# Local-attention mixer: scores as two whole-array fp32r passes on split, stacked heads instead of one plain f32 matmul per half array

## The reference, cut to what matters

```
q = q.reshape(B, nb, BLOCK, SW_KV_HEADS, G, SW_DIM)
kb, vb = band(k), band(v)                    # previous block and this one
s = einsum('bnqgrd,bnkgd->bngrqk', q, kb) * (SW_DIM ** -0.5) + bias
s = where(valid, s, NEG)
p = softmax(concatenate([s, sink], axis=-1), axis=-1)[..., :-1]
o = einsum('bngrqk,bnkgd->bnqgrd', p, vb)
```

## Time and profile before

| | us |
|---|---|
| median of three runs | 2695.01 |
| lowest, highest | 2693.04, 2697.74 |
| profiled execution: span, first to last instruction | 2693.6 |
| mean granted TensorE clock in it | 0.997 of full speed |
| local-attention mixer, from the first score to the last value product | 1585.3 to 1700 |
| the eight tiles' scores begin at | 1585.29, 1598.96, 1615.17, 1627.35, 1639.55, 1651.99, 1664.18, 1676.62 |

### The profile page before, as it was taken

How to read it: one execution, slowest core, us unless ns; L and a number is a source line. 1 busy time by engine, 2 the same in 40 slices (tenths; PEclk the granted TensorE clock), 3 DMA queues, 4 the chain that set the end, 5 groups by cost and what they waited for, 6 DMA issues and landing times.

```text
span 2693.6 us, 32187 instructions
## 1 busy us (share of the span) xinstructions
PE 2653.5 (99%) x12935; PEld 2126.5 (79%) x12935; DVE 1460.7 (54%) x2615; ACT 1122.8 (42%) x1521; POOL 1167.0 (43%) x880
## 2 busy tenths in 40 slices
PE   8999999999999999999999999999999999999998
PEld 7787677778888877778888876888888777888887
DVE  5888556657554145657554145575522565575522
ACT  4544544444333236653333236443333344443332
POOL 3454443335445532335445541354455332454453
PEclk9999999999999999999999999999999999999999
DMA  4224032222223221112223331222233222222232
GB/s 164 79 94 172 1 133 86 70 73 96 106 96 110 104 88 63 63 65 98 104 94 110 109 110 48 79 94 98 106 109 110 94 87 71 94 94 94 94 122 81
DMA packets 46597, 253.44 MB, mean 94 GB/s; under 512 B 4528, under 2 KB 11200, under 8 KB 18928
## 3 DMA queue, kind: packets, MB, share of 16 engines
q1 hardware_dynamic: 35376, 231.92, 24.3%
q10 hardware_dynamic: 11072, 19.47, 2.2%
HBM read 249.21 MB, written 10.55 MB: 96 GB/s over the span
## 4 chain that ended last, share of the span: by engine, by line
PE 92%; DVE 4%; ACT 2%; POOL 1%; issue 1%; DMA 0%; SPq 0%; DVEq 0%; ACTq 0%
PE ring L481 79%; PE ring L978 3%; PE turn L983 2%; PE turn L481 1%; PE out L1022 1%; POOL wlo L1219 1%; PE ring L776 1%; PE ring L645 1%; PE out L792 1%; DVE sp L2238 1%; PE out L1028 0%; DVE e L2206 0%; PE out L1110 0%; ACT whi L1270 0%; DVE z L2241 0%
## 5 line engine op out<-in xcount | busy, mean ns | idle before, releaser
L1219 POOL TENSOR_TENSOR wlo<-raw,whi 128x512 fp32r<-128x512 f32 x840 | 1121.8, 1367 | 1456.9 <-ACT whi L1270 1456.8
L481 PE MATMUL ring<-xh,whi 128*128 128x512 f32 x1888 | 753.4, 399 | 9.3 <-DVE xl L1753 8.4
L481 PE MATMUL ring<-xh,wlo 128*128 128x512 f32 x1888 | 736.6, 390 | 0.0
L481 PE MATMUL ring<-xl,whi 128*128 128x512 f32 x1888 | 736.5, 390 | 0.0
L1270 ACT ACTIVATE whi<-raw 128x2048 fp32r<-128x2048 f32 x215 | 411.3, 1914 | 437.1 <-DMA raw<-in_pieces 421.8
L481 PEld LDWEIGHTS ring<-xh,whi 128*128 128x128 f32 x1888 | 354.9, 188 | 114.9 <-issue 41.1
L481 PEld LDWEIGHTS ring<-xh,wlo 128*128 128x128 f32 x1888 | 354.9, 188 | 75.3
L481 PEld LDWEIGHTS ring<-xl,whi 128*128 128x128 f32 x1888 | 355.2, 188 | 72.3 <-issue 3.4
L2391 DVE SCALAR_TENSOR_TENSOR taps<-u,conv,taps 128x511 f32<-128x511 f32 (+1 forms) x344 | 295.7, 905 | 17.3 <-ACT taps L1695 14.8
L2405 DVE TENSOR_TENSOR u<-ring,r 128x512 f32<-128x512 f32 x168 | 114.4, 687 | 299.7 <-PE ring L481 299.7
L481 PE MATMUL ring<-hh,whi 128*128 128x512 f32 (+1 forms) x693 | 265.3, 383 | 0.0
(11 more groups left out here) (304 smaller groups left out, 3423.0 us busy)
## 6 DMA issues: line engine op xcount, KB each, us to landing
raw<-in_pieces SPq DMA_DIRECT2D x215, 1024.0 KB, 4.8
toep<-diag_store ACTq DMA_DIRECT2D x16, 512.0 KB, 3.6
diag_store<-diag_row ACTq DMA_DIRECT2D x1, 5120.0 KB, 25.6
band_store<-band_row ACTq DMA_DIRECT2D x1, 3072.0 KB, 33.1
h<-in_x SPq DMA_DIRECT2D x4, 512.0 KB, 6.3
wbias<-band_store ACTq DMA_DIRECT2D x4, 512.0 KB, 7.2
raw<-in_pieces SPq DMA_DIRECT2D x4, 256.0 KB, 6.4
result<-h SPq DMA_DIRECT2D x2, 512.0 KB, 3.0
```

Source lines behind the costliest of these rows:

```text
L481: ins = pe.matmul(out, stationary, moving, start=first and n == 0, stop=last and n == 2)
L1219: ins = pool.tensor_tensor(m.wlo[slot][:, part], m.raw[slot][:, part], m.whi[slot][:, part].bitcast(F32), ALU.subtract)
```

## The change

The scores become f32r matmuls over the whole array. For each key head `kd[g]` holds two arrays: its high part, in both partition halves, and its low part, in both halves. For each query head there is one array `qw`: its high part in the head's own partition half, its low part in the other half. Head j's block is then two passes with the same stationary query array, one on the high keys and one on the low keys, summed in PSUM over all 128 partitions.

VectorE takes the keys in one operation a unit into `kn`, ScalarE rounds high parts (2 operations of 64x512 for each key head and each tile's queries), VectorE subtracts for the low parts (again 2 and 2). TensorE waits for `q_low` and `k_low` instead of `pu_taken`. The query arrays of even and odd tiles are kept apart. Tiles 0 and 1 begin after 33 and 46 quanta instead of 30 and 44.

```diff
-          "window": (30, 44, 60, 68, 76, 84, 92, 100)}
+          "window": (33, 46, 60, 68, 76, 84, 92, 100)}
...
-        self.kd = self.at("kd", [P, 4, S], o + 36864)
+        self.kd = [self.at(f"kd{g}", [P, 2, S], o + (36864, 40960, 88064, 92160)[g], F32R) for g in range(4)]
+        self.qw = [[self.at(f"qw0{j}", [P, S], o + 14336 + 16384 * j, F32R) for j in range(2)],
+                   [self.at(f"qw1{j}", [P, S], sq_at + 2048 * j, F32R) for j in range(2)]]
...
+        self.kn = [self.at(f"kn{u}", [P, S], o + 49152 + 3584 * (2 + u)) for u in range(2)]
...
+    def stacked_pair(b, t, i, qs, ks, lo, n):
+
+        for j in range(2):
+            u = 8 * t + 2 * i + j
+            if u < 2:
+                pe.wait_ge(m["unit_taken"], b.at("unit_taken", 0))
+            else:
+                pe.wait_ge(m["su_taken"], b.at("su_taken", u - 1))
+            out, q = m.ring[2 + j][:, 0:n], qs[j][:, i * P:(i + 1) * P]
+            pe.matmul(out, q, ks[:, 0, lo:lo + n], start=True, stop=False)
+            pe.matmul(out, q, ks[:, 1, lo:lo + n], start=False, stop=True).then_inc(m["su_ready"], 1)
...
-                pe.wait_ge(m["pu_taken"], b.at("pu_taken", WINDOW_Q_UNIT[t] + 1))
+                pe.wait_ge(m["q_low"], b.at("q_low", 2 * t + 2))
+                pe.wait_ge(m["k_low"], b.at("k_low", 2 * (t // 2) + 2))
...
-                    score_pair(b, t, i, m.qt[t % 2], m.kd[:, t // 2, :], lo, n)
+                    stacked_pair(b, t, i, m.qw[t % 2], m.kd[t // 2], lo, n)
...
+        def keys_high(g):
+            act.wait_ge(m["pu_taken"], b.at("pu_taken", g // 2 + 1))
+            for to in range(2):
+                act.activation(m.kd[g][64 * to:64 * to + 64, 0, :], m.kn[g // 2][64 * (g % 2):64 * (g % 2) + 64, :],
+                               ACT.Copy).then_inc(m["k_high"], 1)
+
+        def queries_high(t):
+            act.wait_ge(m["pu_taken"], b.at("pu_taken", WINDOW_Q_UNIT[t] + 1))
+            if t >= 2:
+                act.wait_ge(m["su_ready"], b.at("su_ready", 8 * t - 8))
+            for j in range(2):
+                half = slice(64 * j, 64 * j + 64)
+                act.activation(m.qw[t % 2][j][half, :], m.qt[t % 2][half, :], ACT.Copy).then_inc(m["q_high"], 1)
         split_hi(b, 2)
+        keys_high(0)
+        queries_high(0)
         split_hi(b, 3)
+        keys_high(1)
...
+            if t == 0:
+                keys_high(2)
+                keys_high(3)
             hi_at(b, "window", t, 1)
+            if t + 1 < TILES and t != 1:
+                queries_high(t + 1)
             if 2 <= t:
                 take_out(b, t - 2)
             if 1 <= t < TILES + 1:
                 weights(2 * t - 2)
                 weights(2 * t - 1)
+            if t == 1:
+                queries_high(t + 1)
             hi_at(b, "window", t, 2)
...
-                for g in range(2):
-                    src = slice(64 * g, 64 * g + 64)
-                    for to in range(2):
-                        ins = dve.tensor_tensor(m.kd[64 * to:64 * to + 64, 2 * unit + g, :], project_bank(m, unit)[src, :],
-                                                m.r[src, :], ALU.mult)
...
+                take_feature(b, unit, m.kn[unit], 1.0)
+
+        def keys_low(g):
+            dve.wait_ge(m["k_high"], b.at("k_high", 2 * g + 2))
+            half = slice(64 * (g % 2), 64 * (g % 2) + 64)
+            for to in range(2):
+                dve.tensor_tensor(m.kd[g][64 * to:64 * to + 64, 1, :], m.kn[g // 2][half, :],
+                                  m.kd[g][half, 0, :].bitcast(F32), ALU.subtract).then_inc(m["k_low"], 1)
+
+        def queries_low(t):
+            dve.wait_ge(m["q_high"], b.at("q_high", 2 * t + 2))
+            for j in range(2):
+                half, other = slice(64 * j, 64 * j + 64), slice(64 - 64 * j, 128 - 64 * j)
+                dve.tensor_tensor(m.qw[t % 2][j][other, :], m.qt[t % 2][half, :],
+                                  m.qw[t % 2][j][half, :].bitcast(F32), ALU.subtract).then_inc(m["q_low"], 1)
...
         for unit in range(3):
             take(unit)
+        keys_low(0)
+        queries_low(0)
...
             if t == 0:
                 take(3)
+                keys_low(1)
...
             if t < TILES and t != 1:
                 take(t + 5 if t else 4)
+            if t == 0:
+                keys_low(2)
+                keys_low(3)
+                queries_low(1)
             if 1 <= t < TILES + 1:
                 normalise(2 * t - 1)
             if t == 1:
                 take(6)
+            if 1 <= t < TILES - 1:
+                queries_low(t + 1)
             if 2 <= t:
                 take_low(b, t - 2)
```

More of the change, by code:

```diff
@@ L205, in mix @@
         else:
+            t.update(q_high=16, q_low=16, k_high=8, k_low=8)
             t.update(exped=64, sunk=16, lsum=16, rl_ready=16, normed=64)
@@ L2280, in take @@
             else:
-                dve.wait_ge(m["pu_ready"], b.at("pu_ready", unit + 1))
-                for g in range(2):
-                    src = slice(64 * g, 64 * g + 64)
-                    for to in range(2):
-                        ins = dve.tensor_tensor(m.kd[64 * to:64 * to + 64, 2 * unit + g, :], project_bank(m, unit)[src, :],
-                                                m.r[src, :], ALU.mult)
[L2287 to L2290, removed]
+                take_feature(b, unit, m.kn[unit], 1.0)
[11 more added lines that the diff above has]
+                                  m.qw[t % 2][j][half, :].bitcast(F32), ALU.subtract).then_inc(m["q_low"], 1)
         def normalise(h):
```

## The result

The changed kernel takes 2698.69 us (median of 20 runs, 2695.49 to 2701.25) against 2695.16 (20 runs, 2691.51 to 2697.74): a ratio of 1.0014, 95% interval 1.0008 to 1.0021. So it is slower by about 3.5 us, 0.14%, which is under the 0.2% taken as the bound of no change. Forecast were 2696.5 us, no change within 0.2%, and a range of 2687.5 to 2702.5. The case forecast was the right one; the step from it to the number was 2.2 us short.

A forecast was written before the change was run, and what follows sets the result against it. TensorE, busy for 99% of the span, was taken as the bound; a 10.8 us gain against 12.35 us of added waits gave +1.5 us on 2695.0, so 2696.5 us, with an 8-in-10 range of 2687.5 to 2702.5.

The forecast's parts named there:

- The case forecast: Local-attention mixer: TensorE's saving is taken back by waits on other engines, 2696.5 us; chance 0.45.
- gain of TensorE, eight tiles: Score pairs in the mixer: shorter f32r passes save 1.28 us a tile, 10.2 us over eight tiles.
- wait of tile 0 that goes: Tile 0: TensorE's 0.55 us wait for VectorE goes, as eight key copies become two.
- tile 0, piece 2: Before tile 0's scores: three VectorE subtractions delay GpSimd's low part of piece 2, costing 1.0 us.
- tile 1, its query: Before tile 1's scores: TensorE waits for ScalarE's queued copies and VectorE's query subtractions beside GpSimd, costing 3.4 us.
- tile 2, its query: Before tile 2's scores: take, copies and subtractions of its query end late, costing 1.0 us.
- ScalarE's queue, five tiles: Tiles 2 to 6: query copies delay ScalarE's output and transposes copy, 0.85 us a tile, 4.25 in five.
- GpSimd, tiles 2, 4, 6: Tiles 2, 4, 6: the earlier normalisation falls under GpSimd's operations and takes turns with them, costing 2.7 us.
- rival B: Score passes: 128-column f32r runs like plain f32, 0.21 us instead of 0.12, giving 2701.1 us; chance 0.18.
- rival C: Wait before tile 1: TensorE's clock falls, 3.4 us at half costs 1.7, giving 2698.2 to 2699.9; chance 0.12.
- Rival A: Mixer waits stay small, 5.2 us at their low ends, giving 2689.4 us; chance 0.23.
- Rival D: Score passes don't do what is said: one with its bank free still waits for its weights; chance 0.02.

The follow-up runs named there:

- the run with no split: Kernel before with two f32r passes per score block, keys and queries not split into high and low parts: 2687.24 us, ratio 0.9969.
- the starts alone: Kernel before with only tiles 0 and 1 begun after 33 and 46 quanta instead of 30 and 44: 2695.86 us, ratio 0.9996.
- tile 1's query first: Changed kernel with tile 1's query split ahead of the keys of tiles 4 to 7 and piece 4, on ScalarE and VectorE: 2694.66 us, ratio 0.9998.
- three edits: Changed kernel with tile 1's queries first, query high parts of tiles 3 to 7 on VectorE, high parts of pieces 6 and 7 sooner: 2688.02 us.
- tile 1 four quanta later: Changed kernel with tile 1 begun after 50 quanta instead of 46, tiles 2 to 6 one quantum later: 2697.5 us, ratio 1.0006.
- the query's high part on VectorE: Changed kernel with query high parts of tiles 3 to 7 made by VectorE instead of ScalarE: 2692.95 us, ratio 0.9993.
- GpSimd's work moved: Changed kernel with ScalarE making high parts of pieces 6 and 7 one tile earlier, so GpSimd's low parts come sooner: 2695.1 us, ratio 1.0003.

## Why the prediction was right, and where it was short

The forecast's balance was 12.35 of costs against 10.8 of gain. Term by term, with what the trace after and the runs show:

| term | forecast, us | measured, us | where |
|---|---|---|---|
| gain of TensorE, eight tiles | 10.2 | 10.3 | the run with no split, its waits added |
| wait of tile 0 that goes | 0.55 | 0.5 to 0.8 | the starts alone: the stage 0.76 shorter |
| tile 0, piece 2 | 1.0 | 1.1 | wait of 0.95, 1.1 between starts |
| tile 1, its query | 3.4 | 2.8 | wait of 2.65, 2.8 between starts |
| TensorE's clock behind it | 0 | 1.5 | 3.4 us at half; tile 1's query first gives the same |
| tile 2, its query | 1.0 | 1.0 | wait of 0.80, 0.96 between starts |
| ScalarE's queue, five tiles | 4.25 | 5.1 | between starts: 1.07, 0.99, 1.08, 0.90, 1.08 |
| GpSimd, tiles 2, 4, 6 | 2.7 | 2.5 | between starts: 0.43 + 1.30 + 1.28 - 0.5 |
| balance | +1.5 | +2.9 to +3.2 | the stage: +3.25 |

"Between starts" is the time from TensorE's last start before the wait to the first behind it, less what the same step takes with no wait; it is 0.06 to 0.17 us more than the wait that the profile names.

**The gain** came out as its steps had it. The value taken for a 128-column pass, 0.12 us, is 0.11 in the trace; the bound of 0.21 wasn't met, and with it rival B fell: the steps at the two ends of the first pair, 0.06 and 0.17, together are no longer than two ordinary ones.

**Tile 0** is right in place, cause and size. On before's scale (less the 1.97) the scores start at 1588.27; forecast was near 1588.3. A subtraction beside GpSimd took 1.73 us, where 1.70 was taken from the row of another stage; GpSimd paid 0.46 for each, forecast 0.45. The estimate from the Trainium skill's "SBUF — State Buffer" (Who interferes with whom) was 1.85 for such a turn; the trace shows 1.73, so the turns are there as the page has them, a little shorter. That it is the subtractions that make piece 2 late rests on the run with the new starts alone, which has no such wait; no run moved those subtractions.

**Tile 1** starts at 1602.37 on before's scale; forecast was 1603.0. Two errors cancel in part. ScalarE was done 0.4 us later than thought, as its copies are slower; VectorE's two subtractions took 2.37 instead of 3.4: 0.97 more than the 1.40 with GpSimd quiet, about one turn and not two, since GpSimd's first operation (from 1600.78) was nearly done when they began (1601.91).

**What the sum lacked** stands behind this wait. The sum priced the 3.4 us of waiting and took TensorE's clock after it as unchanged; rival C, with a chance of 0.12, had the mechanism right, the price nearly (1.7 for 3.4 us at half, measured 1.5), and its chance too low. The row that bore on it showed the clock at 0.70 behind a shorter gap, 1.68 us, than the one I forecast, 3.4; the row against it is a stretch whose longest gaps are 1.33. The nearer row should have been the sum's: the forecast would have been 2698.2. The Trainium skill's "TensorE: Matmul & The Clock Gate" (Part 1) says that a gap in TensorE's work sets its clock back to half. The trace agrees: it stood at half for 3.4 us behind the wait of 2.65.

Neither of the two rows was as firm as the forecast took it, though. The wait of 1.68 us and the two of some 1.33 stand in all ten traces, and the trace after, in windows as in the earlier trace rows, has the clock the other way round: up behind the first, down behind the second.

```profile
238.00:242.00 4.00, 3.79 (x14) 2.17 (x14) 3.93 (x17) 1.38 (x5) 1.50 (x3) 1.00 1.01 377
308.00:312.00 4.00, 3.59 (x12) 1.42 (x14) 0.69 (x1) 0.87 (x2) 0.83 (x1) 0.57 0.00 0
```

In seven traces (the one before among them) the clock fell behind the 1.68 us, in the other three behind the 1.33. One trace of the kernel before could not show that.

**The mis-sized term** is ScalarE's queue: 0.85 us a tile forecast, 1.02 measured. The mechanism is the one described, wait for wait; the copies were priced by a 128-partition copy out of PSUM, 0.54 from start to start, and take 0.65. Two copies a tile give 0.2 us, all of the difference; over five tiles it is the 0.85 missing. With the clock (1.5), and less the 0.6 that tile 1 was overpriced, this makes 1.75 us, the difference between the balance forecast and the stage's 3.25. The smaller differences of the table cancel. Part of the closeness is luck: tile 1's wait was overpriced by 0.6 us, which hid a quarter of the 2.35 that the clock and ScalarE's copies were underpriced by.

**GpSimd under the normalisation** rested on an assumption, that a scaling with one SBUF input takes turns with GpSimd as well. The scalings of tile 4 show it: 1.84 us for four against 1.07, and 1.08 when GpSimd's work is moved. GpSimd ends at 1651.42, which fits the first of them waiting for its last operation; the sum ahead of them took 0.76 instead of 0.15. And the run without the split shows that this cost belongs to the shorter scores, not to the split.

**Rival A** (the waits stay small) fell: none of the five costs was smaller than its low bound. **Rival D** fell with the first score pair. The listed signs came: tiles 3 and 5 of 11.9 us (forecast 11.7, the 0.2 being ScalarE's copies), a tile 4 of 13.3 (forecast 13), and the second transposes released by ScalarE, 0.9 to 1.1 late (forecast 0.85).

What stays open: the clock. Its worth is counted from the passes of one stretch, and the run that removes the wait agrees; but a kernel that keeps the wait and holds the clock up was not tried, and each kernel was traced once, so it isn't shown that the clock falls behind this wait in every execution.

## What to carry to other kernels

On a kernel whose first engine is 99% busy, price a change by what the other engines must now do between two of its instructions; a faster pass here gave 10.3 us and queues ordered for the slower one took some 14 back, of which 12 came back with three edits to their order and place. Put the work that the bound engine needs next ahead of the work that it needs later (tile 1's query ahead of the keys of tiles 4 to 7), and give added copies to the engine whose queue has room at that moment, not to the one with the lowest total. And price a new wait of TensorE twice, once for itself and once for the clock behind it; starting the consumer later can merely move the wait to the next one, while shortening the chain that feeds it removes it.

## What the hardware showed that was not expected

- **The clock after a wait.** In the four traces of this case with a wait of 2.23 or 2.65 us in the mixer (the changed kernel, tile 1 four quanta later, the query's high part on VectorE, GpSimd's work moved) the granted clock went to half for about 3.4 us, within 1.4 us after the matmuls came back. In the six traces whose waits there stayed at or under 1.65 us it stayed at 1.00. At the front of the program the same wait of 1.68 us was followed by a fall in seven traces and by none in three. So the length of the gap alone does not say it.
- **Short f32r passes.** 128 columns follow each other by 0.11 us, 256 by 0.12. Going from 256 columns to 128 saves next to nothing here.
- **ScalarE's half copies.** A copy of 64 partitions by 512 from SBUF takes 0.65 us from start to start, more than one of 128 partitions out of PSUM (0.54). Half the partitions did not make it cheaper here; the two also differ in where they read, and no run separates that. The same copy on VectorE, with GpSimd quiet, took 0.45:

```profile
1638.83 0.87 DVE L2336 TENSOR_SCALAR qw<-qt 64x512 fp32r<-64x512 f32 x2
```
